# Input and output of a two-layer encoder trunk in transposed layout, and its last output tile in two passes

## What is computed

```python
def rmsnorm(x, w):
    y = x * rsqrt(mean(x * x, axis=-1, keepdims=True) + 1e-6)
    return y * w

def swiglu(x, w_gate, w_up, w_down):          # D_FF = 2816
    return (silu(x @ w_gate) * (x @ w_up)) @ w_down

def reference(x, ...):
    for l in range(2):
        x = x + 0.5 * swiglu(rmsnorm(x, ffn1_norm[l]), ...)
        x = x + hybrid_mixer(rmsnorm(x, mix_norm[l]), ...)   # gated DeltaNet, conv branch, gates
        x = x + 0.5 * swiglu(rmsnorm(x, ffn2_norm[l]), ...)
    return rmsnorm(x, final_norm)
```

## Time and profile before

| | us |
|---|---|
| three runs | 2758.24, 2758.9, 2763.64 |
| median | 2758.9 |
| the profiled execution | 2760.39 |
| its span | 2758.4 |
| TensorE products, busy | 2716.6 (98%) |
| TensorE weight loads, busy | 2265.0 (82%) |
| VectorE, busy | 1588.3 (58%) |
| ScalarE, busy | 1095.7 (40%) |
| GpSimd, busy | 275.3 (10%) |

### The profile page before, as it was taken

The page is one execution under the profiler, slowest core; times in us unless marked ns, Lnnn a source line. Parts: engine busy times, 40 slices in busy tenths (PEclk is TensorE's granted clock), DMA queues, the critical chain, the costliest instruction groups (busy, mean ns, idle before and its releaser), DMA issues.

```text
span 2758.4 us, 35870 instructions
## 1 busy us (share of the span) xinstructions
PE 2716.6 (98%) x13089; PEld 2265.0 (82%) x13089; DVE 1588.3 (58%) x2511; ACT 1095.7 (40%) x1842; POOL 275.3 (10%) x241
## 2 busy tenths in 40 slices
PE   8999999999999999999999999998999999999999
PEld 7888878888888888888888888787888888888887
DVE  5554357878885345553355543687788843455432
ACT  4222246666763232222222222566566632322221
POOL 0000022122120020000000000212122201100000
PEclk9999999999999999999999999999999999999999
DMA  5333337766564333333333334567666553333331
GB/s 154 98 99 105 90 89 143 114 136 129 118 133 100 96 88 102 98 94 96 97 98 99 92 97 87 117 116 118 122 125 132 121 99 93 97 96 95 95 99 65
DMA packets 478060, 292.53 MB, mean 106 GB/s; under 512 B 12060, under 2 KB 462756, under 8 KB 477956
## 3 DMA queue, kind: packets, MB, share of 16 engines
q1 hardware_dynamic: 462820, 236.57, 34.1%
q0 software_dynamic: 14976, 54.53, 10.4%
q10 hardware_dynamic: 160, 0.07, 0.0%
HBM read 234.51 MB, written 2.10 MB: 86 GB/s over the span
## 4 chain that ended last, share of the span: by engine, by line
PE 90%; DVE 4%; DMA 3%; ACT 2%; issue 1%; POOL 0%; SPq 0%; POOLq 0%; ACTq 0%; DVEq 0%
PE bank L456 88%; DMA raw<-in_w_in 1%; DMA w_lo<-raw 1%; PE bank L662 1%; PE bank L610 1%; DVE w_lo L1194 1%; DVE c_lo L1674 0%; ACT w_hi L840 0%; ACT c_hi L1150 0%; DVE mg_lo L1716 0%; DMA xin<-in_x 0%; DVE qa L1367 0%; DVE g_lo L1210 0%; PE bank L698 0%; PE bank L624 0%
## 5 line engine op out<-in xcount | busy, mean ns | idle before, releaser
L1194 DVE TENSOR_TENSOR w_lo<-raw,w_hi 128x1024 fp32r<-128x1024 f32 x343 | 424.0, 1237 | 546.9 <-ACT w_hi L840 546.7
L840 ACT ACTIVATE w_hi<-raw 128x1024 fp32r<-128x1024 f32 x447 | 471.1, 1056 | 671.7 <-PE bank L456 640.3
L456 PE MATMUL bank<-h_hi,w_hi 128*128 128x512 f32 x1504 | 588.8, 391 | 7.6 <-DVE sqb L1374 6.2
L456 PE MATMUL bank<-h_hi,w_lo 128*128 128x512 f32 x1504 | 586.9, 390 | 0.0
L456 PE MATMUL bank<-h_lo,w_hi 128*128 128x512 f32 x1504 | 586.7, 390 | 0.0
L456 PE MATMUL bank<-g_hi,w_hi 128*128 128x512 f32 x928 | 384.4, 414 | 8.8 <-DMA w_lo<-raw 6.5
L456 PE MATMUL bank<-g_hi,w_lo 128*128 128x512 f32 x928 | 379.8, 409 | 0.0
L456 PE MATMUL bank<-g_lo,w_hi 128*128 128x512 f32 x928 | 370.9, 400 | 0.0
L456 PEld LDWEIGHTS bank<-h_hi,w_hi 128*128 128x128 f32 x1504 | 283.0, 188 | 68.1 <-issue 9.4
L456 PEld LDWEIGHTS bank<-h_hi,w_lo 128*128 128x128 f32 x1504 | 283.0, 188 | 59.2
L1462 DVE SCALAR_TENSOR_TENSOR cacc<-c_raw,ncol,cacc 128x512 f32<-128x512 f32 x464 | 330.4, 745 | 0.4
(11 more groups left out here) (261 smaller groups left out, 3390.4 us busy)
## 6 DMA issues: line engine op xcount, KB each, us to landing
raw<-in_w_in SPq DMA_DIRECT2D x128, 512.0 KB, 8.5
w_lo<-raw POOLq DMA_DIRECT2D x104, 512.0 KB, 5.9
raw<-in_ffn_w_gate SPq DMA_DIRECT2D x88, 512.0 KB, 3.7
raw<-in_ffn_w_up SPq DMA_DIRECT2D x88, 512.0 KB, 3.7
raw<-in_ffn_w_down SPq DMA_DIRECT2D x64, 512.0 KB, 4.0
raw<-in_ffn_w_down SPq DMA_DIRECT2D x32, 384.0 KB, 3.4
raw<-in_w_a_out SPq DMA_DIRECT2D x16, 512.0 KB, 4.0
raw<-in_w_b_out SPq DMA_DIRECT2D x16, 512.0 KB, 4.3
```

What stands on the lines that cost most here:

```text
L456: return nc.tensor.matmul(o, a, b, start=start, stop=stop, **kw)
L840: nc.scalar.activation(w_hi[c % SLOTS][:, :], raw[c % SLOTS][:, :], ACT.Copy).then_inc(hi_done, 1)
L1194: tt(w_lo[c % SLOTS][:, :], raw[c % SLOTS][:, :], w_hi[c % SLOTS][:, :].bitcast(F32), ALU.subtract).then_inc(lo_v, 1)
```

## The change

x is handed over as eight chunks of 128 channels x 512 tokens, and the result is handed back in the same layout; the host lays both out. The parameters of a layer come as one array of 128 x 8 x 49, already as the columns of pcol, the final norm's weights among them (PR_FIN).

*The start.* SP issues chunk 0 of x straight into xT, weight unit 0, the chunks 1 to 7, then units 1 to 3. ACT's queue issues the constants' first matrix and the parameters. The 33 turns on TensorE, the copies to f1c and xT and the copies out of the banks are gone. ScalarE: x_hi of chunk 0, unit 0, x_hi of chunks 1 to 7, unit 1 in two halves (half_hi), then the squares with units 2 and 3 between them. VectorE follows with x_rest, lo, and half_lo. GpSimd no longer takes unit 1. TensorE may take the first half of unit 1 when half_lo is raised.

*The parameters.* TensorE's 16 turns of them are gone, and so are VectorE's copies out of the banks; three scalings by 0.5 in place stay.

*The end.* The last tile is made in two passes of 256 tokens (last_down), into banks 5 and 7, 66 products each with the same weights. The last square is no longer added to the sum by GpSimd: TensorE sums both over channels in one accumulation (last_stats). last_stats(0) and last_spread(0), for the first 256 tokens, stand inside the second pass; those of the second half behind it. VectorE's last_norm multiplies each chunk of xT in place by the channel's weight and by the spread factor, 256 tokens at a time. SP stores two chunks of one half per transfer, eight transfers.

The core of the diff:

```diff
-            x_tile(0)
-            x_tile(1)
+            x_chunk(0)
...
                         if first and isinstance(i, int) and c == 0:
-                            x_tile(2)
-                            x_tile(3)
+                            for k in range(1, KT):
+                                x_chunk(k)
...
             def params(l):
-                sp.wait_ge(par_t, l + 1)
-                sp.dma_start(prow[PR_DW:PR_DW + TAPS, :], dw_conv_w[l]).then_inc(par_in, 16)
...
+                sp.wait_ge(hx_done, l * 24)
+                sp.dma_start(pcol[:, :, :], params_in[l]).then_inc(par_in, 16)
...
-            sp.wait_ge(par_t, DEPTH + 1)
-            sp.dma_start(prow[:, :], final_norm.rearrange("(o c) -> o c", o=1).broadcast_to([P, D])).then_inc(par_in, 16)
...
+            for h in range(2):
+                for k in range(0, KT, 2):
+                    sp.wait_ge(fin_y, h * KT + k + 2)
+                    sp.dma_start(out[k:k + 2].rearrange("k p s -> p k s")[:, :, side(h)], xT[:, k:k + 2, side(h)]).then_inc(stored, 16)
...
-                if w == 0 and l == 0:
-                    params(0, 6)
-                elif w == 1 and l < DEPTH - 1:
-                    params(l + 1, 6)
...
+                def last_stats(h):
+                    pe.wait_ge(ssq_done, 3 * DEPTH * 7 + 6)
+                    pe.wait_ge(fin_sq, h + 1)
+                    for c in range(2):
+                        t = slice(h * HALF + c * P, h * HALF + c * P + P)
+                        mm(bank[h][:, c:c + 1], ssq[:, t], ones[:, 0:1], stop=False)
+                        m = mm(bank[h][:, c:c + 1], sqb[1][:, t], ones[:, 0:1], start=False)
+                    m.then_inc(fin_st, 1)
+
+                def last_spread(h):
+                    pe.wait_ge(fin_rs, h + 1)
+                    for c in range(2 * h, 2 * h + 2):
+                        m = nc.tensor.transpose(bank[2 + h][:, c * P:c * P + P], whole(nrm[:, 1, c:c + 1]), ident)
+                    m.then_inc(fin_bc, 1)
+
+                def last_down():
+                    pe.wait_ge(x_upd, l * 24 + (base_upd + 6))
+                    for h in range(2):
+                        for q in range(3):
+                            c = 9 + q
...
+                            a, b = DSPLIT[q]
+                            for k in range(a, b):
+                                w_ = slice((k - a) * P, (k - a) * P + P)
+                                for n, (wt, at) in enumerate(((w_hi, act_hi), (w_hi, act_lo), (w_lo, act_hi))):
+                                    m = mm(bank[5 + 2 * h][:, side(h)], wt[c % SLOTS][:, w_], at[:, k, side(h)],
+                                           start=k == 0 and n == 0, stop=k == FT - 1 and n == 2)
+                            if h and q == 0:
+                                last_stats(0)
+                            elif h and q == 1:
+                                last_spread(0)
+                        m.then_inc(fin_p, 1)
+                    last_stats(1)
+                    last_spread(1)
...
+            act.wait_ge(par_in, 16)
+            first_x(0)
+            hi(0, 0)
+            for k in range(1, KT):
+                first_x(k)
+            act.wait_ge(raw_landed[1], 16)
...
+            nc.scalar.activation(w_hi[1][:, 0:UNIT // 2], raw[1][:, 0:UNIT // 2], ACT.Copy).then_inc(half_hi, 1)
+            nc.scalar.activation(w_hi[1][:, UNIT // 2:], raw[1][:, UNIT // 2:], ACT.Copy).then_inc(hi_done, 1)
...
+                        if end and i == 1 and c == 11:
+                            last_add(0)
+                            last_factor(0)
+                            last_norm(0, range(5))
+                            last_add(1)
+                            last_norm(0, range(5, KT))
+                            last_factor(1)
+                            last_norm(1, range(KT))
+                            break
```

282 lines of the change are left out of this document (125 added, 157 removed).

## The result

| | median us (lowest to highest, runs) | to before, with 95% interval |
|---|---|---|
| before, measured beside it | 2760.3 (2755.1 to 2765.1, 11) | |
| after | 2767.6 (2765.2 to 2772.9, 11) | 1.0027 [1.0017, 1.0037] |

A forecast was written before the change was run, and what follows sets the result against it. TensorE, with 90% of the last-ending chain, was taken as the bound. Start 2.6 + parameters 1.6 + last tile and end 3.7 = 7.9 us, taking the median from 2758.9 to 2751.0 us; range 2747.5 to 2757.5 us.

The forecast's parts named there:

- First product at 9.0 us: Start: TensorE's first dense product begins near 9.0 us, 4.1 us before the old one, with unit 0 landing at about 6.4 us.
- Unit 1: Start: this weight unit lands near 13.4 us, and TensorE reaches it at 15.9 us without a wait.
- 3.0 us at half pace, cost 1.5 us: Start: without turns to raise the clock, the first dense products run 3.0 us at half speed, losing 1.5 us.
- the start: Everything ahead of the first norm: worth 4.1 - 1.5 = 2.6 us, ends 4.2 and 0.5 us.
- Parameters 1.6 us: Two groups of TensorE's parameter turns, 0.79 us each, go: 1.6 us gained, between 1.5 and 1.8 us.
- Last tile and end 3.7 us: From the last tile's products to the span's end: 3.7 us gained, 1.7 at worst, 4.5 at best.
- my upper 0.120: Last tile: products of 256 columns up to 0.120 us apart, not 0.1133, if there is a fixed part; +0.9 us.
- The second add: End: the second half's add starts about 16.7 us after the first short product, behind five last_norm.
- the gap ahead of the sums: End: TensorE idles 1.4 us, too short to lower the clock; otherwise +0.9 us for sums, +0.2 us for turns.
- (c): Rival, last tile: weight loads bound the short products at 0.188 us each; 9.9 us lost, 2760.9 us, no change. Chance 0.06.
- (d): Rival, last tile: 256-column products lose the format's fast form, 0.444 us each; +44 us, 2794.7 us, slower. Chance 0.05.
- the two passes take what the one took: Last down projection: 132 products of 256 columns at 0.1133 us take as long as 66 of 512.

The follow-up runs named there:

- e6: e5 with 20 products of ones on TensorE while it waits for the first weights; 2759.9 us, 0.9995 to before.
- e18: e14 with 20 products of ones on TensorE, in a loop of 5 times 4, while it waits for the first weights; 2753.7 us, 0.9974 to before.
- e5: after with hnw and hnh in one tile, which saves 64 bytes and returns the arena to its old place; 2759.7 us, 1.0000 to before.
- e14: e5 with the end of before (last tile in one pass, result turned, stores in rows); 2754.2 us, 0.9975 to before.
- e11: before with the ready parameter columns alone, 48 of them, so every tile stays where it was; 2758.1 us, 0.9991 to before.
- e1: before with 64 bytes per partition left free behind pcol and nothing else changed; 2767.4 us, 1.0024 to before.
- e17: e14 with the last feed-forward's down projections written out instead of looped, 248 rows more in TensorE's program; 2763.4 us, 1.0008 to before.
- e2: after with 64 more bytes left free behind pcol, 128 bytes in all; 2779.6 us, 1.0070 to before.
- e4: after with 64 bytes left free behind pcol and 64 ahead of the arena, 192 bytes in all for the arena; 2780.7 us, 1.0072 to before.

## Why the prediction was wrong, step by step

**First product at 9.0 us:** 8.62 us. Right; unit 0 landed at 6.1 us instead of 6.4. Unit 1 was there at 12.9 us (13.4 foretold), and TensorE has no gap until the first norm.

**3.0 us at half pace, cost 1.5 us:** the mechanism was right, and e6 and e18 show it: products of ones ahead of the first dense product remove the slow stretch. Its length was mis-sized in the profiled run of after, 5.3 us with twelve products, cost 12 x 0.2 = 2.4 us; in e5 and e14 it was eight products, 3.5 us. So the start is worth 2.0 us in the trace of after and 2.7 in that of e5 (spread at 30.46 us), against 2.6 foretold. The Trainium skill, page "TensorE: Matmul & The Clock Gate", section "What's actually happening", says that the number of slow products at the start changes from run to run of one kernel. No kernel has two traces here; the ten kernels with the new start and no products of ones show between 7 and 12 starts more than 0.4 us apart, which fits. The same page of the Trainium skill, section "Part 4: PE-mode transpose", says that turns do not raise the clock. The trace of after speaks against it, as the earlier trace rows do: with the turns gone, the dense products start slow.

**Parameters 1.6 us:** e11, this part alone, is 0.9991 [0.9981, 1.0000], 2.5 us with 1.6 well inside, but with nothing at the edge. Its trace has 0.9 us for each of the two places, 1.8 us. Right as far as this shows. (Ten small transfers for each layer went, not eleven; nothing hung on it.)

**Last tile and end 3.7 us:** 4.1 us. Short products are 0.1178 us apart in after, between 0.1133 and my upper 0.120: 132 x 0.0045 = 0.6 us dearer. With the arena at its old place (e5) they are 0.1199 us apart, 0.9 us dearer: the fixed part that I put at the end of the range is there, in full. GpSimd's power took 0.71 us instead of 1.02, for two columns instead of four; a last_norm 0.41 and 0.40 us instead of 0.485, so eight of them 3.22 instead of 3.9 us. The second add came 16.9 us after the first short product (2743.87 us), foretold 16.7, and as foretold right behind the five norms, which ended at 2760.66 us. From the second add to the last eight norms it took 3.54 us, foretold 3.6. The clock fell only behind the last sums (granted 0.79 in 2764 to 2766 us), so the gap ahead of the sums, 1.06 us instead of the 1.4 us foretold, did not cost it. Each term was off by some tenths, and they cancel. That the sum of all three parts comes out within 0.2 us (7.7 for 7.9) is luck to that extent: start 0.6 us less, end 0.4 us more.

**Rivals (c) and (d)**, weight-bound or slow short products: did not happen.

**The step that failed** is none of the sum's. It is the silent one: that all that the change does not touch stays as it was, said of the arena's tiles by saying nothing, and of the last down projection by "the two passes take what the one took". Two edits that I read as free were not. "The final norm's weights among them (PR_FIN)" is one column more in pcol; it moved the arena by 64 bytes against the weight slots, and cost 7.9 us (after against e5; e1, the shift alone, 7.3 us). And the two passes in place of the loop's last turn wrote out 322 rows more in TensorE's program. A written-out program of 248 rows more, with nothing else changed, makes the weights of the mixers late and costs 9.3 us in the medians of the pair e14 and e17, 5.1 us in their traces; that the 322 rows do the same is read from the group to which all kernels with the new end belong. So of the three parts' 7.7 us, minus 7.9 and minus about 7 to 9, remains what was measured: 7.3 us slower. None of my rivals was of this sort: the one that ended slower, (d), was of another mechanism, and my 0.01 for "what I don't see" was far too small for a change that moves allocations and unrolls a loop.

The two losses do not add up exactly. After minus before is +7.3 us; -7.7 + 7.9 + 9.3 would be +9.5 us. Medians of one kernel in different groups differ by up to 3 us, which is enough for it.

## What to carry to other kernels

Before pricing an edit, list what it moves that it does not name: the address of every tile behind an allocation that grows, and the length of each engine's program. Where TensorE runs back to back with products of 512 columns, keep the distance of the streamed tile to the weights at a multiple of 256 bytes; a pad line costs nothing, here it was worth 7 to 20 us. For products of 256 columns that distance was the slowest of the four that were measured, so measure there. And where a wait names another engine, look at that engine's own wait in the same microseconds: here VectorE's XT was a late weight transfer twice removed.

## What the runs showed of the hardware

- Products of 128 x 512 in fp32r, each with its own weight load, are 0.2267, 0.2289, 0.2333 and 0.2333 us apart, by the distance of streamed tile and weights' slots modulo 256 bytes (0, 64, 128, 192): up to 3% of these products' time at full clock, with no wait in the trace. The Trainium skill, page "SBUF — State Buffer", section "Operand start alignment", asks only for a multiple of the element size and says that its runs timed nothing; all these places fulfil that rule, and they are not equal in time.
- 248 more written-out rows in TensorE's program, executed 2300 us later, change how long transfers of w_in take (10.9 to 12.6 us) and how busy they keep the DMA engines (22.1 to 30.6%). The packets of 512 bytes stay at 27 ns in the median, and those over 100 ns go from 2.0 to 6.8%. All 20 kernels of the study fall in two groups by these marks, up to 6025 rows and from 6266 on. The cause is open.
- Products of 256 columns in this format are 0.1199, 0.1178, 0.1187 and 0.1135 us apart at the same four distances (first pass of last_down in e5, after, e2 and e4), so not in the order of the long ones. At distance 0, with 0.2267 us for 512 columns, that makes by estimate 0.2136 us for 512 columns and a fixed part of 0.013 us.
- In e6 TensorE worked on products of ones from 1.12 to 7.33 us, then had nothing for 1.41 us; the dense products from 8.74 us on were 0.23 us apart at once.
